# A fused two-layer decoder trunk on one core: another order of the projections, of the norm's steps and of the modulation's matmuls

## The reference, cut to what matters

```python
def _layer(x, c, st, prm):
    mods = (jax.nn.silu(c) @ ada_w + ada_b).reshape(B, 3, 3, 1, D_MODEL)
    def modulate(t, i):
        return t * (1.0 + mods[:, i, 1]) + mods[:, i, 0]
    def residual(t, i, out, w):
        return _layer_norm(ALPHA * t + w * (1.0 + mods[:, i, 2]) * out, ln_g[i], ln_b[i])
    x = residual(x, 0, _swiglu(modulate(x, 0), ffn_wg[0], ffn_wu[0], ffn_wd[0]), 0.5)
    proj = modulate(x, 1) @ w_in
    p_rw, p_gla, p_ml = _split(proj, [RW_PROJ, GLA_PROJ, ML_PROJ])
    ...                                     # three recurrent mixers: RWKV-7, GLA, mLSTM
    mix = jnp.concatenate([o_rw, o_gla, o_ml], axis=-1) @ w_out
    x = residual(x, 1, mix, 1.0)
    x = residual(x, 2, _swiglu(modulate(x, 2), ffn_wg[1], ffn_wu[1], ffn_wd[1]), 0.5)
```

## Time and profile before

| | us |
|---|---|
| median of three runs | 1681.97 |
| lowest and highest of them | 1672.1 and 1684.19 |
| the profiled execution's own time | 1677.3 |
| its span, first to last instruction | 1675.5 |
| PE busy (share of the span) | 1608.5 (96%) |
| DVE busy | 936.3 (56%) |
| ACT busy | 667.0 (40%) |
| POOL busy | 203.6 (12%) |

### The profile page before, as it was taken

One profiled execution on the slowest core, in us unless ns is written; L12 is line 12 of the kernel. 1 busy time (PEld: TensorE's weight loads), 2 busy tenths in 40 slices (PEclk: granted clock), 3 DMA queues, 4 the chain that ended last, 5 costly groups with the idle time before them and its releaser, 6 DMA issues. The chain is left out here.

```text
span 1675.5 us, 32875 instructions
## 1 busy us (share of the span) xinstructions
PE 1608.5 (96%) x14052; PEld 1480.5 (88%) x14052; DVE 936.3 (56%) x1605; ACT 667.0 (40%) x985; POOL 203.6 (12%) x271
## 2 busy tenths in 40 slices
PE   5999999999999999999999999999999999999997
PEld 2999998998767789999989999989877768899996
DVE  1544545586653775555474544466946456655544
ACT  2333334563323355333364333355532334543333
POOL 1000011100222330000110000210022242100011
PEclk9999999999997799999999999999989669999998
DMA  8765555533443174444755545654412116444441
GB/s 310 279 225 209 171 204 204 176 116 100 139 146 104 62 261 143 148 150 151 254 212 198 192 145 173 233 173 138 124 35 84 54 39 244 148 148 148 151 152 68
DMA packets 103864, 268.57 MB, mean 160 GB/s; under 512 B 39560, under 2 KB 42024, under 8 KB 103464
## 3 DMA queue, kind: packets, MB, share of 16 engines
q1 hardware_dynamic: 99304, 263.86, 46.3%
q10 hardware_dynamic: 4416, 2.62, 0.6%
HBM read 260.19 MB, written 6.26 MB: 159 GB/s over the span
## 5 line engine op out<-in xcount | busy, mean ns | idle before, releaser
L2410 DVE TENSOR_TENSOR wlo<-raw,whi 128x1024 fp32r<-128x1024 f32 x300 | 367.6, 1229 | 323.2 <-ACT whi L2261 320.9
L2261 ACT ACTIVATE whi<-raw 128x1024 fp32r<-128x1024 f32 x300 | 316.2, 1055 | 295.3 <-PE psV L2073 262.2
L2071 PE MATMUL psA<-XH,whi 128*128 128x320 f32 x1104 | 345.0, 313 | 7.9 <-DVE wlo L2410 7.5
L2073 PE MATMUL psA<-XH,wlo 128*128 128x320 f32 x1104 | 342.7, 310 | 0.0
L2072 PE MATMUL psA<-XL,whi 128*128 128x320 f32 x1104 | 342.6, 310 | 0.0
L2071 PE MATMUL psV<-XH,whi 128*128 128x320 f32 x848 | 267.1, 315 | 0.2
L2072 PE MATMUL psV<-XL,whi 128*128 128x320 f32 x848 | 263.8, 311 | 0.0
L2073 PE MATMUL psV<-XH,wlo 128*128 128x320 f32 x848 | 263.7, 311 | 0.0
L2071 PEld LDWEIGHTS psA<-XH,whi 128*128 128x128 f32 x1104 | 208.8, 189 | 10.8 <-issue 9.5
L2072 PEld LDWEIGHTS psA<-XL,whi 128*128 128x128 f32 x1104 | 208.7, 189 | 0.3
L2073 PEld LDWEIGHTS psA<-XH,wlo 128*128 128x128 f32 x1104 | 208.7, 189 | 0.0
(11 more groups left out here) (413 smaller groups left out, 2012.1 us busy)
## 6 DMA issues: line engine op xcount, KB each, us to landing
raw<-weights_dram SPq DMA_DIRECT2D x400, 512.0 KB, 3.4
own<-weights_dram SPq DMA_DIRECT2D x56, 512.0 KB, 5.9
in_xh<-weights_dram SPq DMA_DIRECT2D x6, 512.0 KB, 4.2
in_xl<-weights_dram SPq DMA_DIRECT2D x6, 512.0 KB, 5.0
raw<-weights_dram SPq DMA_DIRECT2D x6, 384.0 KB, 3.6
raw<-weights_dram SPq DMA_DIRECT2D x8, 256.0 KB, 3.8
in_hl<-weights_dram SPq DMA_DIRECT2D x4, 512.0 KB, 5.4
ZS<-st_rw_dram SPq DMA_DIRECT2D x2, 768.0 KB, 4.4
```

The source lines that it names most:

```text
L2071: mm(out, split_hi(n)[:, k], hi[:, kt], start=first, stop=False)
L2073: return mm(out, split_lo(n)[:, k], hi[:, kt], start=False, stop=last)
L2261: activation(split_hi(n), buffer(DENSE[n]), ACT.Copy).then_inc(hi_done, 1)
L2410: tt(split_lo(n), buffer(DENSE[n]), split_hi(n).bitcast(F32), ALU.subtract).then_inc(lo_done, 1)
```

## The change

It has three parts.

1. The order of the 20 later projections, the mixer steps `rw` and `rv` and the convolution `cv` is written out in `PROJ_MIXED`, in place of the dealing by weights.
2. The norm: ACT squares the mean out of PSUM; DVE no longer does, and copies the mean only after `var_ready`. The low part of one weight chunk, which DVE made while ACT was at the root, is now made after the second tile's multiplication. In the last norm POOL subtracts the mean from four of the eight tiles.
3. The groups of `ada`: at most two (8 chunks) in a gap, none in layer 1's gap behind `out`, none in layer 1's first up product; 12 groups in place of 7 in layer 0's mixers and 6 in place of 3 in layer 1's; of them 5 (20 chunks) in the steps of `LATE`, where 3 and 2 (12 and 8 chunks) stood. ACT's copy of a group inside a gap ahead of the root (`THREE`) falls away with the third group.

```diff
-RW_PRE = (2, 2, 2, 2, 3, 3, 2, 2, 2)
-RW_TWICE = (3, 5, 7)
-CV_AT = (4, 9, 12, 15, 18)
+PROJ_MIXED = ("rw 23 24 rw 25 26 rw cv 11 12 rw 13 rv 14 cv 15 rw 16 17 cv 27 rw 28 rv 19 cv 20 rw 21 cv 22 rw 29 rv 30 rw").split()
...
-IN_LATE = (3, 2)
+LATE = ("rw ada ml ada gl ada rw ml ada gl ml ada rw gl ada ml ada rw gl ada ml ada gl ada ada rw ada ml ada gl ada ada rw ml ada ada "
+        "gl ada ml ada ada rw fold gl rw ml su mix rs rw rs su hi.0 rs lo.0 rw hi.1 rw hi.2 lo.1 early.0 rw lo.2 early.1 rw").split()
+IN_LATE = (5, 5)
...
     steps, left = layer_plan(0, groups(0, 0, 4, 5) + groups(0, 1, 0, 1, 2, 3),
-                             (groups(0, 1, 4, 5) + groups(0, 2, 0), groups(1, 0, 2, 3), groups(1, 0, 4, 5) + groups(1, 1, 0)),
-                             groups(0, 2, 1, 2, 3, 4, 5) + groups(1, 0, 0, 1))
+                             (groups(0, 1, 4, 5), groups(1, 1, 0, 1), groups(1, 1, 2, 3)),
+                             groups(0, 2, 0, 1, 2, 3, 4, 5) + groups(1, 0, 0, 1, 2, 3, 4, 5))
     out += steps
-    steps, left = layer_plan(1, groups(1, 1, 1, 2, 3), (groups(1, 1, 4, 5) + groups(1, 2, 0), groups(1, 2, 4, 5), []),
-                             groups(1, 2, 1, 2, 3), left)
+    steps, left = layer_plan(1, [], (groups(1, 1, 4, 5), [], []), groups(1, 2, 0, 1, 2, 3, 4, 5), left)
...
                 def norm(s):
                     nc.scalar.preload_act_table_set("natural_log_exp_and_others")
+                    act.wait_ge(sem("mean_full"), 2 * s + 1)
+                    A.do(activation(VR[:], mean_bank[s][:, 0:TOK], ACT.Square), sem("mean_squared"))
+                    act.wait_ge(sem("var_ready"), s + 1)
+                    rsqrt(A, VR[:], sem("sd_ready"))
                     if s in THREE:
                         rows(*THREE[s])
-                    act.wait_ge(sem("var_ready"), s + 1)
-                    rsqrt(A, VR[:], sem("sd_ready"))
...
                             V.do(tt(ZT[:, t], ZT[:, t], VR[:], ALU.mult), sem("zn_ready"))
+                            if t == 1:
+                                split_to(n_next + LOCK - 1)
...
-                        if after is not None and t < DT - 1:
+                        if s is None and DT // 2 - 1 <= t < DT - 1:
+                            vec.wait_ge(sem("centered"), t + 2 - DT // 2)
+                        elif after is not None and t < DT - 1:
                             V.do(tt(ZT[:, t + 1], ZT[:, t + 1], MN[:], ALU.subtract))
...
                 def norm(s):
-                    bank = fV.take()
-                    V.do(nc.vector.tensor_copy(MN[:], bank[:, 0:TOK]), sem("bankV_free"))
-                    V.settle()
-                    V.do(tt(VR[:], MN[:], MN[:], ALU.mult))
-                    V.settle()
-                    bank = fV.take()
-                    V.do(tt(VR[:], bank[:, 0:TOK], VR[:], ALU.subtract), sem("bankV_free"))
+                    mean = fV.take((sem("mean_full"), 2 * s + 1))
+                    bank = fV.take((sem("mean_full"), 2 * s + 2))
+                    vec.wait_ge(sem("mean_squared"), s + 1)
+                    V.do(tt(VR[:], bank[:, 0:TOK], VR[:], ALU.subtract))
                     V.settle()
                     V.do(ts(VR[:], VR[:], 0.0, LN_EPS / ALPHA ** 2, ALU.max, ALU.add), sem("var_ready"))
-                    V.do(tt(ZT[:, 0], ZT[:, 0], MN[:], ALU.subtract))
-
-                    split_to(n_next + LOCK - 1)
+                    V.do(nc.vector.tensor_copy(MN[:], mean[:, 0:TOK]), sem("bankV_free"))
+                    V.settle()
+                    V.mark(sem("mean_ready"))
+                    V.do(tt(ZT[:, 0], ZT[:, 0], MN[:], ALU.subtract), sem("bankV_free"))
+
                     vec.wait_ge(sem("sd_ready"), s + 1)
...
+                pool.wait_ge(sem("mean_ready"), 3 * DEPTH)
+                for t in range(DT // 2, DT):
+                    G.do(nc.gpsimd.tensor_tensor(ZT[:, t], ZT[:, t], MN[:], ALU.subtract), sem("centered"))
```

More of the change, by code:

```diff
@@ L89 @@
 LEVELS = (6, 6, 3)
-RW_PRE = (2, 2, 2, 2, 3, 3, 2, 2, 2)
-RW_TWICE = (3, 5, 7)
-CV_AT = (4, 9, 12, 15, 18)
+PROJ_MIXED = ("rw 23 24 rw 25 26 rw cv 11 12 rw 13 rv 14 cv 15 rw 16 17 cv 27 rw 28 rv 19 cv 20 rw 21 cv 22 rw 29 rv 30 rw").split()
 RW_INVERSE = 9 + 2 * (max(LEVELS) - 1)
 GL_FIRST, ML_FIRST = 3, 4
-LATE = ("rw ml ada gl rw ml ada gl ml ada_ rw gl ml ada rw gl ml ada ada_ gl ada rw ml ada_ gl ada rw ml ada gl ada_ ml ada rw fold "
-        "gl rw ml su mix rs rw rs su hi.0 rs lo.0 rw hi.1 rw hi.2 lo.1 early.0 rw lo.2 early.1 rw").split()
-IN_LATE = (3, 2)
+LATE = ("rw ada ml ada gl ada rw ml ada gl ml ada rw gl ada ml ada rw gl ada ml ada gl ada ada rw ada ml ada gl ada ada rw ml ada ada "
+        "gl ada ml ada ada rw fold gl rw ml su mix rs rw rs su hi.0 rs lo.0 rw hi.1 rw hi.2 lo.1 early.0 rw lo.2 early.1 rw").split()
+IN_LATE = (5, 5)
 EARLY_FIRST = 5
@@ L169, in ada_bursts @@
               for n, group in enumerate(groups)]
-    return bursts + [[("fold", *groups[-1])]]
+    return bursts + [[("fold", *group)] for group in groups[-1:]]
 def gap_groups(groups):
@@ L196, in layer_plan @@
     out += steps
-    rest = [("proj", L, t) for t in PROJ_ORDER[NRW:]]
-    for k in CV_AT:
-        rest.insert(k, ("cv", L))
     out += after([("proj", L, t) for t in PROJ_ORDER[:NRW]], left)
-    out += spread([slot for k, w in enumerate(RW_PRE)
-                   for slot in ([(("rw", L), 1), (("rv", L), w - 1)] if k in RW_TWICE else [(("rw", L), w)])], rest)
+    out += [("proj", L, int(name)) if name.isdigit() else (name, L) for name in PROJ_MIXED]
     rw, gl, ml = [("rw", L)], [("gl", L)], [("ml", L)]
@@ L208, in layer_plan @@
     for name in LATE:
-        if name == "fold" or name == "ada_" and IN_LATE[L] < 3:
-            continue
-        if name not in ("ada", "ada_"):
+        if name not in ("ada", "fold"):
             out.append((name.split(".")[0], L, *map(int, name.split(".")[1:])))
@@ L214, in layer_plan @@
         out.append(chunks.pop(0))
-        while chunks and chunks[0][0] == "fold":
+        while len(chunks) > 1 and chunks[0][0] == "fold":
             out.append(chunks.pop(0))
@@ L661, in hybrid_trunk @@
         half_bank, proj_bank = {}, {}
-        var_bank = {}
+        var_bank, mean_bank = {}, {}
         low_bank = {}
@@ L2181, in norm @@
                     pe.wait_ge(sem("z_ready"), (s + 1) * DT)
-                    mm(means[0][:, 0:TOK], con("mean1024", P), ZT[:, DT - 1], start=False, stop=True).then_inc(sem("bankV_full"), 1)
+                    mean_bank[s] = means[0]
+                    mm(means[0][:, 0:TOK], con("mean1024", P), ZT[:, DT - 1], start=False, stop=True).then_inc(sem("mean_full"), 1)
                     pe.wait_ge(sem("sq_ready"), (s + 1) * DT)
-                    mm(means[1][:, 0:TOK], con("mean1024", P), SQ[:, DT - 1], start=False, stop=True).then_inc(sem("bankV_full"), 1)
+                    mm(means[1][:, 0:TOK], con("mean1024", P), SQ[:, DT - 1], start=False, stop=True).then_inc(sem("mean_full"), 1)
                 pe.wait_ge(sem("c_ready"), 2)
```

## The result

The changed kernel takes 1682.4 us (median of 20 executions, 1673.9 to 1690.4), the kernel before 1675.6 (20 executions, 1671.1 to 1686.8). The ratio is 1.0038, 95% interval 1.0022 to 1.0054: slower by 0.4%, 6.4 us, where I forecast 10.2 us less. The profiled execution of the changed kernel took 1686.6 us (span 1684.7), that of before 1677.3 (1675.5), both at a mean granted clock of 0.958.

A forecast was written before the change was run, and what follows sets the result against it. PE, busy 96% of the span, was taken as the bound. The terms -8.8, -2.2, +4.2, -8.2 and +4.8 sum to -10.2 us on 1677.3, 1667.1, stated as 1668; range 1653 to 1684.

The forecast's parts named there:

- B: Norms: the changed norm, over the gaps and the last norm, gains 2.2 us; bounds -4 and +4.
- E: Both layers' mixers: 32 chunks of `ada` more, +4.8 us; bounds -8 and +19.5.
- A: Later projections: the new order removes PE's stall and the low clock behind it in both layers, -8.8 us.
- Three are taken like the first (-0.3 each), the last gives -1.3: Gaps at the norms: four gaps shorten by these amounts against the old ones; with +0.8 elsewhere, -1.4 us together.
- are done before DVE needs the last: Last norm: POOL's four subtractions, at 0.88 us, finish in time; the last norm nets -0.8 us.
- C: Emptier gaps: 2.6 us idle in four, bringing the low clock in three, +4.2 us; bounds 0 and 11.
- D: Layer 1's first up product and gap behind `out`: chunk bursts and folds taken away, -8.2 us.
- the two layers are an experiment that the kernel makes by itself: Mixers' first stretches: comparing layer 0 (16 chunks, 71.13 us) with layer 1 (4, 67.71) prices a chunk at 0.29 us.
- E's late part: Mixers' late stretches: 8 chunks more in layer 0 cost 2.3 us, 12 more in layer 1 give -0.9.
- the clock rival: Mixers' late stretches: 20 chunks lift the granted clock to near 1, mixers -8 us, sum 1655 to 1657; chance 0.22.
- The mixers hide nothing: Mixers: each chunk costs 0.61 us as anywhere, 19.5 us in place of 4.8, total 1683; chance 0.18.
- The pause behind the table load: Norms: a pause of the load's own length puts 1.3 us on each of six norms, total 1676; chance 0.05.

The follow-up runs named there:

- order_and_plan: The changed kernel with the norm of the kernel before put back; ratio 0.9981 to the kernel before, 3 us less.
- norm_alone: The kernel before with only the changed norm, plan and order of projections as before; ratio 1.0076 to the kernel before, 12.7 us more.
- no_pool_end: The changed kernel without POOL's four subtractions in the last norm, DVE doing all eight; ratio 1.0025 to the kernel before.
- square_only: The changed kernel with the split back ahead of the root wait and all eight last subtractions on DVE; ratio 0.9997 to the kernel before.
- order_alone: The kernel before with only the written-out order of the projections; ratio 0.9963 to the kernel before, 6.2 us less.
- late_fill: The kernel before with the new projection order and late mixer chunks raised from 12 to 20 (layer 0), 8 to 12 (layer 1); ratio 0.9940.
- late_thin: The changed kernel with the matmuls of the 40 late chunks cut from 256 columns to 16; ratio 1.0059 to the kernel before.
- late_double: The changed kernel with the matmuls of the 40 late chunks issued twice; ratio 1.0035 to the kernel before.

## Why the prediction was wrong

Two terms of the sum failed: B, the norm, which cost 9.6 us and was forecast to gain 2.2, and E, the chunks in the mixers, forecast at +4.8 with about +15 left for it. The other terms came out near their forecasts.

**A, order: right.** No stall near the last projections, 6.2 us less by the ratio (-8.8 forecast, interval 1.5 to 10.7). In the changed kernel's profile the stretches are 2.9 us shorter, and that with 3.7 us lost to new low clock behind emptied gaps, which C counts.

**B, norm: the timeline right, the term wrong in sign.** The changed kernel's gaps are 7.3 to 7.8 us from the last `SQ` matmul, which starts within 0.1 us of the table load (7.3 computed). Gaps and end together measured +0.6 (-2.2 forecast), but in the gaps two edits cancel: the emptied plan took 5.8 us out of them (38.2 to 32.4, order_and_plan) and the norm put 5.0 back. The step that failed is the one that set them against the old gaps: "Three are taken like the first (-0.3 each), the last gives -1.3". Those gaps held three groups, or a late load, and were long for that. order_and_plan shows what they are once emptied with the old norm: 6.3 us, but 7.3 behind layer 0's out product. The one fair comparison was that last gap, which had two groups all along and which I had priced at +0.8; norm_alone has it at 7.3 against 6.4. So the norm costs 5 us in the gaps, and 9.6 in all by the ratios. The last norm was forecast at -0.8 and gave +1.4. The missed step is the sentence that POOL's four subtractions "are done before DVE needs the last": they are, but they double DVE's own. I had named the contention and left it out of the sum. no_pool_end gives 0.9 of the 1.4 to it; the other 0.5 stays without POOL's part and with the split put back (13.6 us in square_only, 13.0 with the old norm), so it is the square's.

**C, the low clock behind the gaps: right in size.** Forecast +4.2 in three gaps. It came anew in two (timelines below), for 8.3 us, in which PE loses 0.12 of each 0.27: 3.7 us.

**E, the mixers: the term that was too small.** Forecast +4.8. With A, C, D, the gaps and the end taken at what they measured, about +15 is left of the +6.4 (the 3 us of the norm's cost that lie neither in the gaps nor in the end are in it). In the profile it lies in the mixers. The failed step is "the two layers are an experiment that the kernel makes by itself", from which came 0.29 us for a chunk: layer 1's first stretch in the kernel before had a clock of 0.91 and layer 0's 1.00, so the slow layer with few chunks was made to look dear, and a chunk cheap. Where both sides had the full clock, a chunk cost 5.0/12 = 0.42 us in layer 0's first stretch (before and changed), 0.67 (order_alone and late_fill), and, with layer 1's 54.9 us in the changed kernel, (62.5 - 54.9)/12 = 0.63 between the layers.

**E's late part and the clock rival.** Forecast +1.4 for 20 chunks more (2.3 and -0.9); the profiles show +9.9 and +9.5. The same price of 0.29 stood in the one, and the guess that layer 1's stretch becomes like layer 0's in the other. By the fit 20 chunks are +15 at equal low clock, and of the other 4 us nearly all goes with 9 us more of low clock in layer 0. I had the clock either rise to near 1 or not at all. late_thin and late_double show a third way: the clock moves with the matmuls, and their time and its gain cancel. The late stretches take 91 us in one execution and 99 to 102 in another of the same placement, with 31 and with 51 to 55 us of low clock; why the low clock lasts longer in one of them is not shown. What a chunk brings besides columns (its loads, its wait for `psC`, its fold and copies) was never taken away alone: its 0.29 us is the fit's.

**D: right.** Layer 1's first up product -7.0 us, and no L2082 in it.

**The rivals.** "The mixers hide nothing" came nearest in the time (1683), partly by luck: for the late chunks its price of 0.61 is near what the fit gives, but its sum has the norm at -2.2 and nothing for what the clock pays back. The pause behind the table load was not seen: the load of 624.11 took 1.28 and the square began at 625.40. The Trainium skill's drain of about 1.38 us (ScalarE: Activation LUTs, What ACT_TABLE_LOAD costs) does not show in this trace either.

**Behind the gaps.** PE's first tile behind the first gap, behind the third, and behind the last:

```profile
294.37 0.38 PE L2062 MATMUL psA<-XH,xhi 128*128 128x320 f32 x1 [3.09 <-DVE XL L2456]
...
870.24 0.38 PE L2062 MATMUL psA<-XH,xhi 128*128 128x320 f32 x1 [3.09 <-DVE XL L2456]
...
1437.42 0.60 PE L2062 MATMUL psA<-XH,xhi 128*128 128x320 f32 x1 [6.55 <-DVE XL L2456]
1437.82 0.47 PE L2063 MATMUL psA<-XL,xhi 128*128 128x320 f32 x1
1438.09 0.47 PE L2064 MATMUL psA<-XH,xlo 128*128 128x320 f32 x1
```

Matmuls ran 0.27 us apart for 3.2 us behind the first gap, 5.1 behind the fourth and 4.5 behind the last, where the kernel before had about 5 already; behind the other two there were none. The first and the third gap ended with the same 3.09 us of idle time, and only the first brought low clock. So I can't tell from the idle time alone whether it comes.

## What to carry to other kernels

When one edit empties a place and another changes what bounds it, price each against the kernel that has the other one already: the old gap was long for its third group, and the norm got the credit for taking it out. Before a piece of work goes to another engine's queue, ask what the first engine did while that queue was blocked: here DVE worked through ACT's table load, and afterwards stood idle for 2.5 us until one square was there. Two stretches can't be used to price a piece of work until both ran at the same clock: here 0.29 us came out where 0.42 to 0.8 was true.

## What the runs showed of the hardware

- Matmul columns put into or taken out of a stretch with a clock between its two levels were paid for by the clock: 0.944, 0.958 and 0.970 in the mean (late_thin, changed, late_double), with medians of 1684.9, 1682.4 and 1682.3 us. That is this kernel's late steps; in the first stretch, at a clock of 1.00 (0.97 thinned), taking out the columns of 28 chunks saved 4.7 us.
- In the changed kernel's last norm, POOL's `tensor_tensor` beside DVE's of 128x320 makes DVE's 0.96 to 1.20 us instead of 0.48, and POOL's own 1.01 instead of 0.88.
- The record of the granted clock and the matmuls' spacing agree: in the changed kernel they run 0.27 us apart from 1437.8 to 1442.35, and the windows 1438 to 1442 and 1443 to 1448 have a clock of 0.50 and 1.00.
- Low clock costs length: in the late stretches of 13 profiles 0.42 to 0.43 us for each us at the lower level, by the fit.
